# Moving 18 gate products into the state-space stage of a hybrid decoder step, and reordering VectorE's work in the sample stage

## What is computed

```python
h = rmsnorm(x, g) * (1 + sc1) + sh1
proj = h @ w_in                        # u (512), q, k, v (768 each)
y, hr, hi = s5_scan(u, ...)            # 32 groups of 16 channels, 64 complex states
y = gelu(y); y = y * sigmoid(y @ w_glu)
attn = merge of three dilated windows  # prompt: over itself; samples: over caches
gates = sigmoid(h @ w_mgate + b_mgate) # 2048 columns
g_ssm, g_attn = split(gates, 2)
out = (g_ssm * (y @ w_br_ssm) + g_attn * (attn @ w_br_attn)) @ w_out
x = x + gt1 * out
x = x + gt2 * moe(rmsnorm(x) ...)      # 32 experts, top 2 of the best group
y_out = rmsnorm(x, g_final)
```

## Time and profile before

| what | us |
|---|---|
| median of three runs | 1731.17 (1728.9 to 1735.99) |
| the profiled execution | 1739.92 |
| its span, first to last instruction | 1736.9 |
| PE busy | 1562.5 |
| DVE busy | 511.1 |
| ACT busy | 279.6 |
| POOL busy | 112.1 |
| sample stage | 559.7 to 886.1 |
| state-space stage | 886.1 to 1082.4 |
| merge of the branches | 1082.4 to 1182.7 |
| experts | 1182.7 to 1682.3 |
| last block | 1682.3 to 1736.9 |

### The profile page before, as it was taken

How to read it: one execution, slowest core, us unless ns; L and a number is a source line. 1 busy time by engine, 2 the same in 40 slices (tenths; PEclk the granted TensorE clock), 3 DMA queues, 4 the chain that set the end, 5 groups by cost and what they waited for, 6 DMA issues and landing times. The chain is left out here.

```text
span 1736.9 us, 20316 instructions
## 1 busy us (share of the span) xinstructions
PE 1562.5 (90%) x8509; PEld 1047.9 (60%) x8509; DVE 511.1 (29%) x1064; ACT 279.6 (16%) x633; POOL 112.1 (6%) x113
## 2 busy tenths in 40 slices
PE   5999999999998969999987998999998699999950
PEld 3566579898787646776665665666887333333310
DVE  4300001101442470103613702443355332111107
ACT  3100000001444201101123101000122011111103
POOL 0000000000120320000010000000000000000013
PEclk9899999998665988879986558999998699999985
DMA  9332422200451332113103000842102689999848
GB/s 318 102 118 73 140 81 86 66 10 25 189 212 36 119 97 94 39 50 132 62 21 52 1 0 15 291 155 100 52 25 110 259 302 383 415 416 414 350 177 242
DMA packets 128300, 253.16 MB, mean 146 GB/s; under 512 B 22457, under 2 KB 93769, under 8 KB 120002
## 3 DMA queue, kind: packets, MB, share of 16 engines
q1 hardware_dynamic: 99842, 186.52, 30.3%
q0 software_dynamic: 10560, 33.50, 5.8%
q10 hardware_dynamic: 17808, 31.86, 5.0%
HBM read 204.96 MB, written 49.63 MB: 147 GB/s over the span
## 5 line engine op out<-in xcount | busy, mean ns | idle before, releaser
L966 PE MATMUL psum<-h_t,ring 128*128 128x352 f32 x768 | 249.3, 486 | 5.1 <-PEq L623 2.7
L966 PEld LDWEIGHTS psum<-h_t,ring 128*128 128x128 f32 x768 | 153.1, 202 | 92.0 <-issue 17.2
L351 PE MATMUL psum<-h_t,ring 128*128 128x352 f32 x576 | 174.4, 465 | 2.7 <-DVE h_t L510 2.7
L369 PE MATMUL psum<-ring,h_t 128*128 128x256 f32 (+1 forms) x720 | 171.8, 397 | 0.0
L369 PEld LDWEIGHTS psum<-ring,h_t 128*128 128x128 f32 (+1 forms) x720 | 155.0, 284 | 12.9 <-issue 2.4
L351 PEld LDWEIGHTS psum<-h_t,ring 128*128 128x128 f32 x576 | 110.2, 192 | 65.7 <-issue 6.6
L1924 PE MATMUL psum<-ring,big 128*128 128x256 f32 (+1 forms) x576 | 131.2, 387 | 2.1 <-PEq L1617 2.1
L1924 PEld LDWEIGHTS psum<-ring,big 128*128 128x128 f32 (+1 forms) x576 | 105.3, 185 | 23.1 <-issue 3.2
L2011 PE MATMUL psum<-w_gate_up,u_rows 128*32 128x512 f32 x608 | 101.7, 609 | 3.2 <-ACT u_rows L2132 1.1
L2011 PE MATMUL psum<-ring,u_rows 128*32 128x512 f32 x576 | 101.7, 599 | 1.7 <-ACT u_rows L2132 0.9
L2033 PE MATMUL psum<-big 128*32 128x512 f32 x736 | 83.7, 595 | 0.8 <-DVE big L2424 0.8
(11 more groups left out here) (455 smaller groups left out, 1852.2 us busy)
## 6 DMA issues: line engine op xcount, KB each, us to landing
big<-in_w_exp_down SPq DMA_DIRECT2D x32, 1024.0 KB, 10.7
ring<-in_w_ada SPq DMA_DIRECT2D x24, 1024.0 KB, 7.3
w_gate_up<-in_w_exp_gate SPq DMA_DIRECT2D x13, 1024.0 KB, 15.0
w_gate_up<-in_w_exp_up SPq DMA_DIRECT2D x13, 1024.0 KB, 19.9
ring<-in_w_exp_gate SPq DMA_DIRECT2D x13, 1024.0 KB, 7.3
ring<-in_w_exp_up SPq DMA_DIRECT2D x13, 1024.0 KB, 9.4
tmp_expert_rows<-ring POOLq DMA_DIRECT2D x12, 1024.0 KB, 4.4
ring<-in_w_in SPq DMA_DIRECT2D x11, 1024.0 KB, 8.5
```

Of the source, the lines that this page charges most:

```text
L351: m = nc.tensor.matmul(bank[(e + j) % NB][:, 0:CW], w[:, k, c * P:(c + 1) * P], ht3[:, k, j * CW:(j + 1) * CW], start=(k == 0), stop=(k == ...
L369: m = nc.tensor.matmul(bank[e % NB][0:rows_of(t), 0:WB], lhs, w[:, k, :], start=(k == 0), stop=(k == KT - 1))
L966: m = T_.matmul(bank[4 + u % 4][:, 0:CW], w_[:, k, c0:c0 + P], ht3[:, k, j * CW:(j + 1) * CW], start=(k == 0), stop=(k == KT - 1))
```

## The change

1. 30 of the 48 gate units stay in the sample stage: "start" 2, "params" 1, "c_h0" 3, five in each group ("turn_probs" 1, "next" 0), "merge" 5, "merged" 4.
2. The other 18 (six blocks of 128 channels by three ranges) are made in the state-space stage by new functions `late` on PE and ACT: seven between the tap groups, five between the inject products, three before the outputs and one after each of the first three quarters. Their weights come in six loads of 512 KB on SP into tiles that are free there; two output buffers take them to memory. `b_bar` and `c_cols` become one tile, and the sample outputs of both halves share one bank, at partitions 0 and 32.
3. All gates are stored with the bias alone (Identity in place of Sigmoid), and ACT applies the sigmoid in the merge, in place, between the load and DVE's multiply.
4. DVE makes the query pairs first. Powers, B-bar and the real table follow in groups 0, 1 and 2, after the copy of the turned probabilities; the imaginary table follows after the groups.
5. The last block is joined to the expert block: its instructions follow on each engine without the barrier, POOL's gathers wait for a semaphore of ACT, and SP loads `g_final` once all gate-up products are made.

```diff
-        FILL = {"start": 2, "params": 2, "c_h0": 9, "merge": 6, "merged": 8}
+        FILL = {"start": 2, "params": 1, "c_h0": 3, "merge": 5, "merged": 4}
-            FILL.update({f"scores{g}": 1, f"turn_scores{g}": 1, f"turn_probs{g}": 2, f"values{g}": 1, f"rows{g}": 1, f"next{g}": 1})
+            FILL.update({f"scores{g}": 1, f"turn_scores{g}": 1, f"turn_probs{g}": 1, f"values{g}": 1, f"rows{g}": 1, f"next{g}": 0})
...
                         V.tensor_copy(pt2[0:NS, 2, :], bank[1][0:NS, 256:384]).then_inc(s_pte, 1)
+                        (powers, b_bar, b_table_re)[g]()
                         dve.wait_ge(s_oa, g + 1)
...
                     V.memset(merge[1][:, TT - 5].rearrange("p g h d -> p (g h d)"), 1.0).then_inc(s_clr, 1)
+                    b_table_im()
...
-                            A.activation(g_sb[:, u % GB, :], bank[4 + u % 4][:, 0:CW], ACT.Sigmoid,
+                            A.activation(g_sb[:, u % GB, :], bank[4 + u % 4][:, 0:CW], ACT.Identity,
...
+        LATE = 3 * len(LATE_TRIPLES)
+        TAPS_FILL, INJECT_FILL = (1, 1, 1, 1, 1, 1, 1, 0), (0, 0, 1, 0, 0, 1, 0, 0, 1, 0, 0, 1, 0, 0, 1, 0)
+        SCAN_FILL, Y_FILL = 3, (1, 1, 1, 0)
+        LATE_BANK = [2 + i % 2 for i in range(12)] + [5, 2, 3] + [5] * 3
...
                     sp.dma_start(d_row, I["ssm_d"].to_broadcast([SSM_C, SSM_W])).then_inc(s_dl, 16)
+                    load_late(0)
                     sp.wait_ge(s_usz, 1)
...
+                    sp.wait_ge(s_ut, 8)
+                    for i in range(1, 4):
+                        load_late(i)
                     sp.wait_ge(s_gd, 1)
...
+                    load_late(4)
+                    sp.wait_ge(s_lgt, 3)
+                    load_late(5)
                     sp.wait_ge(s_v, SP2)
...
+                    def late(n):                       # on TensorE
+                        for i in range(late_done[0], late_done[0] + n):
+                            w_, j = late_w[i // 3], i % 3
+                            pe.wait_ge(s_lw[i // 3], 16)
+                            same = [x for x in range(i) if LATE_BANK[x] == LATE_BANK[i]]
+                            if same:
+                                pe.wait_ge(s_lgc, same[-1] + 1)
+                            for k in range(KT):
+                                m = T_.matmul(bank[LATE_BANK[i]][:, 0:CW], w_[:, k, :], ht3[:, k, j * CW:(j + 1) * CW],
+                                              start=(k == 0), stop=(k == KT - 1))
+                            m.then_inc(s_lgt, 1)
+                        late_done[0] += n
...
                     m.then_inc(s_ust, 1)
+                    pe.wait_ge(s_ue, 9)
...
                         m.then_inc(s_g, 1)
+                        late(TAPS_FILL[i])
...
                         m.then_inc(s_v, 1)
+                        late(INJECT_FILL[n])
+                    pe.wait_ge(s_we, SP2)
+                    late(SCAN_FILL)
...
+                                        o = bank[4][32 * r:32 * r + DEC_B, j * P:j * P + DEC_T * SSM_C]
...
                             m.then_inc(s_y if smp == 0 else s_ys, 1)
+                        late(Y_FILL[q])
...
+                    for u in range(8 * CH):            # on ScalarE, in the merge
+                        act.wait_ge(s_gl5[u % GL], 32 * (u // GL + 1))
+                        A.activation(sg[:, u % GL, :, :], sg[:, u % GL, :, :], ACT.Sigmoid).then_inc(s_sg5, 1)
...
-                        dve.wait_ge(s_gl5[u % GL], 32 * (u // GL + 1))
+                        dve.wait_ge(s_sg5, u + 1)
...
                 act.wait_ge(s_yst[0], 16 * ((ROUNDS + 1) // 2))
+                act.sem_inc(s_rows, 1)
...
+                pool.wait_ge(s_rows, 1)
+                for t in range(NT + AHEAD):
```

More of the change, by code:

```diff
@@ L1113, in _ @@
[L1113 to L1122, removed]
@@ L1297, in build @@
         s_dve4 = sem("dve_chain4")
+        LATE = 3 * len(LATE_TRIPLES)
+        TAPS_FILL, INJECT_FILL = (1, 1, 1, 1, 1, 1, 1, 0), (0, 0, 1, 0, 0, 1, 0, 0, 1, 0, 0, 1, 0, 0, 1, 0)
+        SCAN_FILL, Y_FILL = 3, (1, 1, 1, 0)
+        assert sum(TAPS_FILL) + sum(INJECT_FILL) == 12 and SCAN_FILL + sum(Y_FILL) == LATE - 12
+        LATE_BANK = [2 + i % 2 for i in range(12)] + [5, 2, 3] + [5] * 3
+        s_lw = [sem(f"late_gate_w{i}_loaded") for i in range(len(LATE_TRIPLES))]
+        s_lgt, s_lgc, s_lgst = (sem("late_gate_in_psum"), sem("late_gate_ready"), [sem(f"late_gate_stored{i}") for i in range(2)])
         with ExitStack() as st:
@@ L1331, in _ @@
                     sp.wait_ge(s_fo, 64)
+                    for i in range(2):
+                        sp.wait_ge(s_lgst[i], 16 * (LATE // 2))
                 @block.gpsimd
@@ L1390, in _, with late @@
                     T_ = nc.tensor
+                    late_done = [0]
+                    def late(n):
+                        for i in range(late_done[0], late_done[0] + n):
+                            w_, j = late_w[i // 3], i % 3
[7 more added lines that the diff above has]
+                            m.then_inc(s_lgt, 1)
+                        late_done[0] += n
                     for i in range(8):
@@ L1823, in load_down, with at_of @@
             sp.dma_start(w_dn[i], I["w_exp_down"][0, e].rearrange("(k p) f -> p k f", p=P)).then_inc(s_wdn[i], 16)
+        AHEAD = 3
+        s_gf, s_first, s_both, s_mx, s_sq8, s_m8, s_rt8, s_y8, s_os8 = (
+            sem("g_final_loaded"), [sem(f"first_rows{t}_gathered") for t in range(NT)], [sem(f"second_rows{t}_added") for t in range(NT)],
+            sem("x3_ready"), sem("x3_squares"), sem("x3_mean_square"), sem("x3_root"), sem("y_ready"), sem("y_stored"))
+        s_dve8, s_rows = sem("dve_chain8"), sem("all_rows_stored")
+        gr = [big[:, 7232 + 1024 * t:8256 + 1024 * t] for t in range(NT)]
+        sq8 = ring_all[:, 0:D]
+        ss8 = sb("ss8", [P, NT])
+        g_row = row_p["gate1"]
+        def at_of(t):
+            return slice(TILES.index(t), TILES.index(t) + 1)
         with nc.Block() as block:
@@ L2176, in _ @@
                 act.wait_ge(s_yst[0], 16 * ((ROUNDS + 1) // 2))
+                act.sem_inc(s_rows, 1)
+                for t in range(NT):
+                    r = rows_of(t)
+                    act.wait_ge(s_mx, t + 1)
+                    if t:
+                        act.wait_ge(s_sq8, t)
+                    nc.scalar.activation(sq8[0:r, :], x2_of(t)[0:r, :], ACT.Square, accum_out=ss8[0:r, t:t + 1]).then_inc(s_sq8, 1)
+                    act.wait_ge(s_m8, t + 1)
+                    nc.scalar.activation(ss8[0:r, t:t + 1], ss8[0:r, t:t + 1], ACT.Sqrt).then_inc(s_rt8, 1)
             @block.vector
```

186 lines of the change are left out of this document (99 added, 87 removed).

## The result

The changed kernel takes 1675.78 us (median of four runs, 1674.65 to 1686.48), beside 1733.58 for the kernel before on the same chip (1728.9 to 1740.51). The ratio is 0.9672, with a 95% interval of 0.9625 to 0.9719: faster by 3.3%. The forecast was 1725, in a range of 1700 to 1748. The profiled execution of the changed kernel is the longest of its four.

The account below looks back on a forecast made before the run. PE was taken as the bound, busy 1562.5 of 1736.9 us. Sample stage -82.1, state-space stage +77.5, other parts -2 gave -6.6: 1733.3 profiled, less 8.7 for the runs' median, 1725 us; range 1700 to 1748.

Parts of the forecast that it names:

- (i): Output products of the state-space stage: three units among them cost 20.1, warm beginnings return 10, sample outputs 3; together +7.1 us.
- (f): Tap products of the state-space stage: seven units at 6.7 us between them, taps giving back 5.6; together +41.3 us.
- (g): Inject products of the state-space stage: five units between them at 4.9 us each, +24.5 us.
- Rival (A): Taps and outputs: dense units at short distances keep PE's clock up; 1672 us in full, 1698 for half; chance 0.18.
- (h): Before the output products: three units cost +14.2 us and the 10.3 us wait there goes.
- (B): Taps and outputs: the clock never gives anything back, ten units at 7.9 us, +28, 1753 us; chance 0.14.
- The sample stage: Stage that loses 18 gate units and has DVE's work reordered: forecast sum -82.1 us, bounds -93 and -65.
- (c): Cache transposes of group 0: DVE makes queries first, so the wait goes, -13.0, and the next unit starts warm, -2.2 us.
- (D): Group 1 of the sample stage: POOL's tables hold DVE's copies, +9 us, 1734; chance 0.05.
- Column groups: Output stretch: sample outputs of the two halves in different array columns of one bank overlap partly, -3 us.
- (C): Merge stage: sigmoids come between load and multiply and PE waits for them, +19 us, 1744; chance 0.07.
- the end: Block boundary before the expert gathers: removing it gives -1, loading the final gain ahead another -1 us.

Follow-up runs that it names:

- number 5: Changed kernel with all six last gate units ahead of the output products, none among them, and sample products in two banks in turn: 1677.66 us, 0.9668.
- 6: As number 5, with each chunk's sample products right behind its prompt products (two loops swapped): 1673.88 us, 0.9668.
- number 8: Kernel before with two dense dummy units ahead of the outputs, sample products in two banks in turn, halves at partitions 0 and 32: 1696.23 us, 0.9761.
- number 1: Kernel before with two dense dummy units put in PE's pause ahead of the output products: 1723.81 us, 0.9934.
- number 4: Changed kernel with all seven tap units behind the first tap group, none between the other groups: 1679.08 us, 0.9674.
- number 2: Changed kernel with the three units among the output products moved ahead of them, six before and none between: 1709.63 us, 0.9835.
- number 10: Changed kernel with 33 units early and 15 late: one more at the parameters, two more ahead of the merge, none ahead of the outputs: 1665.04 us, 0.9625.
- 11: As number 10, with the last of the five inject units moved behind the inject products: 1660.43 us, 0.9591.
- number 3: Changed kernel with the three units ahead of the outputs moved among the taps, and PE waiting for all four scanned quarters before the outputs: 1704.63 us, 0.9839.
- 7: As number 5, with one wait for ACT put back behind the third quarter's sample products: 1685.49 us, 0.9690.
- 12: As 11, with the first of the seven tap units moved ahead of the sample transposes: 1653.78 us, 0.9547.
- number 9: Kernel before with VectorE's new order alone (queries first, powers, B-bar and tables in pieces), all 48 units staying: 1712.75 us, 0.9865.

## Why the prediction was wrong

**The step that failed is (i).** It took "2.5 for each of four beginnings" as what the upper level gives back, and 6.7 for each unit; +7.1, measured -25.7. The three units cost 5.00 each, and the products went from 98.1 to 57.4 us. The bound of 39 us that the step itself worked out was reached; the value was taken from the wrong reading of a row. The earlier trace rows show the output products at 0.50 for 93.7 us. I read that as products that cannot stay at the upper level. They show only that such products do not climb: they stood behind a wait of 10.3 us and never found the upper level. Numbers 5, 6 and 8 show that they hold it as long as PE does not pause, number 1 shows it for a quarter, and number 4 shows it for the tap products.

**(f) failed by the same reading**, by 10.9 us: seven units cost 7.43 and six times 5.00, 37.4 in place of 46.9; the tap products gave back 7.0 where 5.6 were taken.

**A pause makes the fall possible, not certain.** Behind the last tap group PE waits 0.68 us for ACT, in all these kernels. The changed kernel first, then number 4:

```profile
865.60 0.66 PE L1501 MATMUL psum<-ident,ring 128*128 128x128 f32 x4 [0.68 <-ACT big L1407]
866.58 1.17 PE L1513 MATMUL psum<-u_t,w_sb 128*64 128x136 f32 x8 [0.32 <-ACT w_sb L1416]
```
```profile
861.69 0.66 PE L1501 MATMUL psum<-ident,ring 128*128 128x128 f32 x4 [0.68 <-ACT big L1407]
862.66 0.68 PE L1513 MATMUL psum<-u_t,w_sb 128*64 128x136 f32 x8 [0.32 <-ACT w_sb L1416]
```

In the profiled executions of the changed kernel and of numbers 2, 10 and 11 the level was down within 2 us of that wait, in those of 3 to 7 and 12 it stayed up, and the changed kernel and numbers 2, 5, 6, 7, 10 and 11 have the same work on PE around it. What decides between them no run here shows. In the changed kernel this fall is why (g) measured +26.0 for +24.5: the first inject unit cost 6.02. That such falls are a part of what spreads the runs of one kernel is likely, but with one trace of each it is not shown.

**Rival (A) had the time, and only half of the mechanism.** Worked out at 1672 in full (its own terms, -20 and -34 from 1725, give 1671), with a chance of 0.18, it came within 5 us. But it said that dense units at short distances keep the clock up. Among the taps they keep nothing (number 4: all seven in front, no cost). Among the outputs the first of them keeps the level only because it covers the wait for ACT, which two banks do as well without any unit (number 5). So what the change brought there is: the wait of 10.3 us before the outputs closed by dense work (step (h), whose own +3.9 was right, at +4.1), and the only wait inside covered. (B) is out, since no late unit but the first (7.43) and one of 6.02 cost more than 5.00.

**The sample stage came out as argued**: -85.6 for -82.1, with the wait for the merge at 10.22 for 10.7 and the one for the state rows at 4.82 for 5. The parts agree as well: up to the cache transposes -26.4 (forecast -26.1), the groups -42.4 (-39.6), the tail -16.8 (-16.4), the last unit of the groups counted with the tail. (c) alone, in number 9, is worth -22.0 in its stage (303.6 to 281.6) and -17.7 by the medians, not -15.2: the wait and the next unit are right, and 6.8 more come from groups that ran longer at the upper level in that execution. In the changed kernel five units at 4.88 leave 18.0 of the groups' 42.4 for it. Why the level falls later in the groups I did not test.

**(D) did not happen.** Group 1's copies from PSUM ran beside POOL's tables at the pace of the earlier trace rows, 1.29 us for two:

```profile
643.71 1.29 DVE L1172 COPY big<-psum 128x512 f32<-128x512 f32 x2 [0.15 <-PE psum L997]
```
```profile
643.85 3.85 POOL L953 TENSOR_TENSOR big<-b_bar_c,powers 128x2048 f32<-128x2048 f32 x1
```

By the rule of the Trainium skill (SBUF — State Buffer, "Who interferes with whom") these copies should not be held, and the trace agrees.

**Column groups gave nothing.** (i) took -3 for them. At 0.50 the 48 records of a quarter's sample products take 6.67 us in two banks at one place (before, 1012.85 to 1019.52) and 6.67 in two column groups of one bank (number 2, 989.37 to 996.04). The Trainium skill (TensorE: Matmul & The Clock Gate, "Part 3: Packing small matmuls — row/col tiling") lets such products overlap; this trace does not show it for these, in which three products to each half stand together.

**(C) and the end.** No PE wait for the sigmoids; from the merge's first transpose to the first gather it is 1.0 us more in all. At the end, taking the boundary away gained nothing: the last row store is issued at 1625.68 and the first gather starts at 1631.10, 5.4 us later, where it was 4.05 with the boundary. The gather waits for the store to land either way; the forecast of -2 came out as +1.4 there and -0.4 behind it.

## What to carry to other kernels

Where a stretch of sparse matmuls runs at half clock, ask whether it fell to that level or only began at it: look at the row before its first product. Put dense work right ahead of it, and then hunt every wait of TensorE inside it, even one under a microsecond, since the level may fall there and stays down until dense work comes; a second PSUM bank for a tiny product was worth 30 us here. Work moved to fill a wait pays twice when sparse products follow. One trace does not tell how often the level falls: look at the spread of the runs too.

## What was not expected of the hardware

Tap products (64 rows, 16 and 112 columns) held the granted clock at 1.00 for 16 us, and the output stretch, a third of whose products have 128 rows, for 53; neither lifted it from 0.50, in 24.3 and 93.7 us. Among the output products a pause of 0.82 to 1.15 us went with a fall to 0.50 in all four traces that have one there at the upper level (numbers 1, 2, 7 and 10), during the pause or up to 3 us behind it. Until the last output product the level stayed down, except in number 10, where a unit of 6.95 us raised it.

The fall does not always come: the 0.68 us behind the taps were followed by one in four traces of ten, and after the 0.82 us behind the last output products, where transposes and then the dense products of the gate of y follow, those products began at 0.50 in the changed kernel and at 1.00 in number 5. A wait of 0.60 us ahead of the first output product (number 8) did no harm, nor did waits of 0.79 and 0.95 (number 3) with a dense unit behind them.

Not all tiny products hold: the value products of the sample stage, 128 rows by 4 columns, slow down without a pause, from 1.09 to 1.87 us in the first group of the kernel before, and in the second group of all of these kernels from 2.03 to 3.57 or 3.58 for twice as many. In which block of them it happens differs from trace to trace; in number 5 the first group had none. Where the line between the two kinds lies is open.
